# Linear attention in pairs of chunks, and the state space output a half tile later

## What is computed

```python
def gla_chunked(q, k, v, log_a):          # 4 heads, DK 128, DV 256, CHUNK 64
    b = cumsum(log_a) within a chunk
    q_in = qc * exp(b - b_ref);  k_in = kc * exp(b_ref - b)
    o_intra = where(mask, q_in @ k_in.T, 0) @ vc
    q_inter = qc * exp(b);  k_state = kc * exp(b_last - b)
    # over the chunks, one after the other:
    o = q_inter @ state
    state = exp(b_last) * state + k_state.T @ vc
    return o_intra + o
```

## Time and profile before

| | us |
|---|---|
| median of 3 runs (lowest, highest) | 2891.02 (2888.39, 2895.56) |
| the profiled run | 2889.62 |
| its span, first to last instruction | 2887.9 |
| mean granted clock of TensorE | 0.981 |

### The profile page before, as it was taken

One profiled execution on the slowest core, in us unless ns is written; L12 is line 12 of the kernel. 1 busy time (PEld: TensorE's weight loads), 2 busy tenths in 40 slices (PEclk: granted clock), 3 DMA queues, 4 the chain that ended last, 5 costly groups with the idle time before them and its releaser, 6 DMA issues.

```text
span 2887.9 us, 36253 instructions
## 1 busy us (share of the span) xinstructions
PE 2703.7 (94%) x12891; PEld 2135.1 (74%) x12891; DVE 1811.9 (63%) x3282; ACT 953.3 (33%) x1231; POOL 850.7 (29%) x546
## 2 busy tenths in 40 slices
PE   4999899999777999999999999999998999899997
PEld 2455344699656999999999887698666777588875
DVE  5843754899897787878887898530118633360532
ACT  2324232333465223323233222543233233332221
POOL 2100001255201344434444321243112234244442
PEclk8999999999999999999999999999999999899998
DMA  8511334333235899898998897226223532122221
GB/s 333 181 49 61 115 142 142 134 120 121 109 153 210 291 323 314 308 316 309 315 319 303 294 310 260 97 87 122 71 76 121 158 110 87 59 95 95 95 95 59
DMA packets 191363, 502.57 MB, mean 174 GB/s; under 512 B 30800, under 2 KB 79984, under 8 KB 189216
## 3 DMA queue, kind: packets, MB, share of 16 engines
q1 hardware_dynamic: 141680, 317.30, 32.9%
q0 software_dynamic: 49584, 184.04, 18.0%
HBM read 454.42 MB, written 46.86 MB: 174 GB/s over the span
## 4 chain that ended last, share of the span: by engine, by line
PE 63%; issue 17%; DVE 11%; POOL 5%; DMA 1%; DVEq 1%; ACT 1%; POOLq 0%; ACTq 0%
PE psum L1621 18%; PE psum L1608 14%; PE psum L1907 14%; PE psum L541 6%; PE psum L526 6%; POOL l_r L845 4%; DVE arena L1955 2%; DVE arena L1952 2%; DVE look_oh L1952 2%; DVEq L1955 1%; DVE arena L1959 1%; PE psum L1348 1%; PE psum L1914 1%; DVE arena L2298 1%; DVE arena L2299 1%
## 5 line engine op out<-in xcount | busy, mean ns | idle before, releaser
L870 ACT ACTIVATE arena<-psum 128x512 f32<-128x512 f32 (+7 forms) x486 | 327.3, 686 | 1185.4 <-PE psum L1608 386.3
L1952 DVE TENSOR_TENSOR arena<-arena 128x384 f32<-128x384 f32 (+6 forms) x390 | 307.7, 794 | 496.3 <-ACT arena L870 268.8
L845 POOL TENSOR_TENSOR l_r<-arena,l_r 128x1024 fp32r<-128x1024 f32 x144 | 351.6, 2442 | 704.7 <-ACT l_r L485 704.7
L1621 PE MATMUL psum<-e_r,e_r 128*128 128x512 f32 x2304 | 539.0, 390 | 1.8 <-DVE e_r L1952 1.8
L1608 PE MATMUL psum<-e_r,e_r 128*128 128x384 f32 x2048 | 526.2, 337 | 7.9 <-issue 3.5
L1621 PEld LDWEIGHTS psum<-e_r,e_r 128*128 128x128 f32 x2304 | 431.1, 188 | 89.4 <-DVE e_r L1952 2.5
L870 ACT ACTIVATE e_r<-arena 128x1024 fp32r<-128x1024 f32 x256 | 270.3, 1057 | 360.5 <-PE psum L1621 336.1
L1608 PEld LDWEIGHTS psum<-e_r,e_r 128*128 128x128 f32 x2048 | 371.4, 189 | 20.2 <-POOL l_r L817 6.9
L1608 PE MATMUL psum<-e_r,l_r 128*128 128x384 f32 x1024 | 344.4, 336 | 0.0
L829 POOL DMA_INDIRECT arena<-in_up,arena x128 | 163.5, 1277 | 276.3 <-DVE arena L2424 144.6
L829 POOL DMA_INDIRECT arena<-in_down_rows,arena x128 | 164.0, 1281 | 250.8 <-DVE arena L1959 123.6
(11 more groups left out here) (226 smaller groups left out, 3425.4 us busy)
## 6 DMA issues: line engine op xcount, KB each, us to landing
arena<-in_down SPq DMA_DIRECT2D x128, 512.0 KB, 4.3
arena<-in_up SPq DMA_DIRECT2D x128, 512.0 KB, 6.6
arena<-in_w_ada POOLq DMA_DIRECT2D x48, 512.0 KB, 6.7
scratch_gates<-arena SPq DMA_DIRECT2D x12, 2048.0 KB, 6.3
arena<-scratch_gates SPq DMA_DIRECT2D x32, 768.0 KB, 9.5
arena<-in_w_in SPq DMA_DIRECT2D x44, 512.0 KB, 3.3
arena<-in_w_query SPq DMA_DIRECT2D x16, 512.0 KB, 3.3
arena<-in_w_glu SPq DMA_DIRECT2D x16, 512.0 KB, 3.2
```

The lines of the kernel that those rows point to most:

```text
L845: nc.gpsimd.tensor_tensor(rr(lo, 1024, "l"), reg(RING + q % NSLOT * SLOT, 1024), rr(hi, 1024, "l").bitcast(F32), ALU.subtract).then_inc(S[ ...
L870: do(sc.activation(out, in_, f, **kw), sem)
L1621: last = mm(bank(2 * tt_ + hf), rr(w__ + tt_ * P, P), rr(x__ + hf * 512, 512), start=(first and n == 0), stop=(final and n == 2))
L1952: do(v.tensor_tensor(out, a, b, op), sem)
```

## The change

Linear attention takes two chunks of 64 together as one block of 128 (`GDB`, 4 pairs behind the meta tokens). The factors of the reference hold inside a chunk, so a pair's scores are made of three pieces per head: the two diagonal blocks from `QIN` and `KIN`, and the cross block, queries of the second chunk against keys of the first, from `PQ` and `PK`, which carry the factors to and from the chunk's border. Then DVE multiplies the first chunk's keys by the decay of the second, and the second chunk's queries by that of the first (`gla_dec`), so that both serve for the whole pair; the state decays by the product of both (`dec2`). Scores have a step of their own (`gla_scores`), transposes another (`gla_turn`). The output's transposes go to banks 3 and 4. Steps are seven half units apart.

In the state space stretch the output Y, its transposes, the end step and what follows them come one half tile later; on DVE, scan and states come ahead of the ogla tile's product, and the end step behind the states.

```diff
+GDB = [(0, META)] + [(META + 2 * GC * c, 2 * GC) for c in range(T // GC // 2)]
+NGD = len(GDB)
...
-        GLA_A = {3 * c + 1: c for c in range(len(GCH))}
-        GLA_B = {3 * c + 3: c for c in range(len(GCH))}
-        GLA_C = {3 * c + 5: c for c in range(1, len(GCH))}
-        S5_STEP = [{3 * u + n: u for u in range(S5G // GP)} for n in range(8)]
+        GLA_A = {7 * c - 4: c for c in range(1, NGD)}
+        GLA_T = {7 * c - 3 if c else 1: c for c in range(NGD)}
+        GLA_B = {7 * c - 1 if c else 3: c for c in range(NGD)}
+        GLA_C = {7 * c + 1: c for c in range(1, NGD)}
+        S5_STEP = [{3 * u + n: u for u in range(S5G // GP)} for n in (0, 1, 2, 4, 5, 6, 7)]
...
-                    act_(o, bank(5).rearrange("p (m t) -> p m t", m=8)[:, :, 0:L], ACT.Copy, "~o_set")
+                    act_(o, PS[:, 1536:2560].rearrange("p (m t) -> p m t", m=8), ACT.Copy, "~o_set")
...
+            def gla_scores(c):
+
+                t0, L = GDB[c]
+                pe.wait_ge(S["sm"], S.base("sm") + c - 1)
+                for h in range(GLH):
+                    q, k = h * T2 + t0, h * T2 + t0
+                    mm(bank(5)[:, h * P + GC:h * P + L], reg(KIN + k, L), reg(QIN + q + GC, GC), start=True, stop=True)
+                    mm(bank(5)[0:GC, h * P + GC:h * P + L], reg(PK + k, GC), reg(PQ + q + GC, GC), start=True, stop=True)
+                    last = mm(bank(5)[0:GC, h * P:h * P + GC], reg(KIN + k, GC), reg(QIN + q, GC), start=True, stop=True)
+                last.then_inc(S["gla_sc"], 1)
+
+            def gla_turn(c):
+
+                t0, L = GDB[c]
                 if c >= 2:
+                    pe.wait_ge(S["o_set"], S.base("o_set") + c - 1)
+                elif c:
+                    pe.wait_ge(S["vtok"], S.base("vtok") + c)
                 for m in range(8):
                     last = T_(PS[0:L, 1536 + m * P:1536 + (m + 1) * P], reg(PVV + m * T2 + t0, L), P)
+                if c < NGD - 1:
+                    pe.wait_ge(S["ktok"], S.base("ktok") + c)
+                    if c:
+                        pe.wait_ge(S["gla_dec"], S.base("gla_dec") + c)
+                    for h in range(GLH):
+                        last = T_(bank(2)[0:L, h * P:(h + 1) * P], reg(PK + h * T2 + t0, L), P)
                 last.then_inc(S["gla_tr"], 1)
...
-                        mm(o, reg(SM + h * GC, L, L), reg(VTOK + h * DV, DV, L), start=True, stop=False)
+                        mm(o, reg(SM + h * P, P), reg(VTOK + h * DV, DV), start=True, stop=False)
                         last = mm(o, reg(PQ + h * T2 + t0, L), reg(ST + h * DV, DV), start=False, stop=True)
...
-                    last = T_(bank(5)[:, m * GC:m * GC + L], reg(OTOK + m * P, P, L), L)
+                    last = T_(PS[:, 1536 + m * P:1536 + (m + 1) * P], reg(OTOK + m * P, P), P)
...
+            for c, (t0, L) in enumerate(GDB):
                 if c:
                     wait("gla_sc", c)
+                    tt(k1, k1, bc(dec[:, :, 2 * c:2 * c + 1], [P, GLH, GC]), ALU.mult, FREE)
+                    tt(q2, q2, bc(dec[:, :, 2 * c - 1:2 * c], [P, GLH, GC]), ALU.mult, "gla_dec")
...
                 if s % 2 and name == "ogla":
...
-                if s in S5_STEP[1]:
-                    s5_scan(S5_STEP[1][s])
                 if s in S5_STEP[4]:
                     s5_end(S5_STEP[4][s])
-                if s in S5_STEP[2]:
-                    s5_states(S5_STEP[2][s])
```

More of the change, by code:

```diff
@@ L1217, in _ @@
                     c = GLA_B[s]
-                    L = GCH[c][1]
                     wait("x_spilled", 16)
@@ L1772, in gla_a @@
-                if c:
-                    pe.wait_ge(S["sm"], S.base("sm") + c - 1)
-                    if c >= 3:
-                        pe.wait_ge(S["o_set"], S.base("o_set") + c - 2)
-                    for h in range(GLH):
-                        last = mm(bank(5)[0:L, h * GC:h * GC + L], reg(KIN + h * T2 + t0, L), reg(QIN + h * T2 + t0, L),
-                                  start=True, stop=True)
-                    last.then_inc(S["gla_sc"], 1)
+                if c < NGD - 1:
[4 more added lines that the diff above has]
+                        last = T_(bank(2)[0:L, h * P:(h + 1) * P], reg(PK + h * T2 + t0, L), P)
@@ L2546, in _ @@
             tt(K4, K4, E4, ALU.mult, "gq")
-            for c, (t0, L) in enumerate(GCH):
-                wait("gla_tr", c + 1)
-                do(v.tensor_copy(reg(KTOK, 512, L), bank(2)[0:L]), "ktok")
+            dec2 = reg(DEC2, 16).rearrange("p (h c) -> p h c", h=GLH)
+            tt(dec2, dec[:, :, 1:9:2], dec[:, :, 2:9:2], ALU.mult)
+            sm3 = reg(SM, 512).rearrange("p (h q) -> p h q", h=GLH)
+            sc3 = bank(5).rearrange("p (h q) -> p h q", h=GLH)
+            do(v.memset(A[GC:P, SM:SM + 512].rearrange("p (h q) -> p h q", h=GLH)[:, :, 0:GC], 0.0))
+            for c, (t0, L) in enumerate(GDB):
                 if c:
                     wait("gla_sc", c)
-                    tt(reg(SM, 256, L).rearrange("p (h l) -> p h l", h=4),
-                       PS[0:L, 2560:2816].rearrange("p (h l) -> p h l", h=4),
-                       bc(causal[0:L, 0:L].unsqueeze(1), [L, 4, L]), ALU.mult, "sm")
-                if c < len(GCH) - 1:
+                    k1 = reg(PK, 4 * T2).rearrange("p (h t) -> p h t", h=GLH)[:, :, t0:t0 + GC]
+                    q2 = reg(PQ, 4 * T2).rearrange("p (h t) -> p h t", h=GLH)[:, :, t0 + GC:t0 + L]
+                    tt(k1, k1, bc(dec[:, :, 2 * c:2 * c + 1], [P, GLH, GC]), ALU.mult, FREE)
+                    tt(q2, q2, bc(dec[:, :, 2 * c - 1:2 * c], [P, GLH, GC]), ALU.mult, "gla_dec")
+                    if c >= 2:
+                        wait("gla_o", c - 1)
+                    tt(sm3[:, :, GC:L], sc3[:, :, GC:L], bc(causal[:, GC:L].unsqueeze(1), [P, GLH, GC]), ALU.mult, FREE)
+                    tt(sm3[0:GC, :, 0:GC], sc3[0:GC, :, 0:GC], bc(causal[0:GC, 0:GC].unsqueeze(1), [GC, GLH, GC]),
+                       ALU.mult, "sm")
+                if c < NGD - 1:
+                    wait("gla_tr", c + 1)
+                    do(v.tensor_copy(reg(KTOK, 512, L), bank(2)[0:L]), "ktok")
                     wait("gla_st", c + 1)
@@ L2562, in _ @@
                         else:
-                            stt(st, st, dec[:, h, c:c + 1], new, ALU.mult, ALU.add, "st")
-            wait("gla_o", 8)
+                            stt(st, st, dec2[:, h, c - 1:c], new, ALU.mult, ALU.add, "st")
+            wait("gla_o", 4)
             do(v.memset(reg(TT_, 1024), 0.0), "tt_zero")
@@ L2636, in _ @@
                 name, m = half_stage(s)
+                if s in S5_STEP[1]:
+                    s5_scan(S5_STEP[1][s])
+                if s in S5_STEP[2]:
+                    s5_states(S5_STEP[2][s])
                 if s % 2 and name == "ogla":
```

58 lines of the change are left out of this document (27 added, 31 removed).

## The result

The changed kernel takes 2848.93 us (median of 4 runs, 2844.75 to 2850.61), the kernel before, run beside it, 2893.29 (4 runs, 2888.39 to 2895.97): a ratio of 0.9846, 95% interval 0.9828 to 0.9865. It is faster by 44.4 us, or 1.5%. Forecast were 2845 us and a range of 2836 to 2857. The profiled run after took 2850.61 us, with a span of 2848.9.

What follows compares the result with a forecast made beforehand. PE was taken to bound the kernel, busy 94% of the span, with some 19 us of waits in the state space stretch. Terms -34.1 - 9.5 - 1.7 = -45.3 on 2889.6, plus 1.4 for the median, gave 2845 us, range 2836 to 2857.

Steps and rivals of the forecast that it cites:

- PE bounds, linear attention goes only by work: Linear attention stretch, 168.0 us: PE is busy in all of it, so time goes only if PE work goes.
- The term of -34.1: Linear attention: taking chunks in pairs cuts PE work from 75.3 to 41.2 us, bounds -33 to -36.
- a gap behind L1755: Linear attention: no gap from a 128x128 product to 128x64 transposes, read as a sign against a price for width changes.
- Changes of tile width empty the array: Rival, chance 0.08: in the pairs' scores each width change costs 0.15 to 0.17 us, 5 us in all; time 2849.
- The K transposes wait for nothing: Linear attention: K's transposes, now behind two DVE scaling products, cost nothing; up to 3 us if the cover fails.
- The 0.02 for a low clock by that wait: Rival "Slower", chance 0.02: PE falls to the lower clock in linear attention at the new wait before K's transposes.
- The wait passes to S and falls to 8.8: State space stretch: waits for H move from Y to S, most Z2 waits go; 18.3 to 8.8, -9.5 us.
- The wait only moves to S: Rival, chance 0.12, state space stretch: all 18.3 us of waits return, the clock loss too; time 2856.9.
- all waits go: Rival, chance 0.08, state space stretch: the 18.3 us of waits and 5.1 of clock loss vanish; time 2833.5.
- The clock gives 1.7 back: State space stretch: of two clock losses, 1.7 and 3.4 us, the first comes back and the second does not.
- one stretch of low clock, not two: Sign for the new profile, behind the z and r stretch: only one stretch at the lower clock remains.
- The sum: Whole kernel: -34.1 - 9.5 - 1.7 = -45.3 us, giving 2845.

Runs made afterwards that it cites:

- e1: The changed kernel with the state space part taken back, so the attention pairs alone: 2854.94 us, ratio 0.987 to the kernel before.
- e7: The changed kernel with swap product Z1 ahead of output Y in half units that have both: 2844.31 us, ratio 0.984 to the kernel before.
- e5: The changed kernel with a pair's scores grouped by weight width, four 128x128 products first, then eight 128x64: 2845.47 us, ratio 0.9837 to the kernel before.
- e8: The kernel before with output products reordered in pairs of heads, two of 64 rows, then two of 128: 2890.09 us, ratio 0.9991.
- e3: The kernel before with only the later state space steps, old DVE order kept: 2889.16 us, ratio 0.999.
- e4: The kernel before with only the new DVE order, old table of steps kept: 2890.43 us, ratio 0.999.
- e2: The kernel before with the state space part alone (later steps and new DVE order): median 2888.82 us, ratio 0.9986.
- e10: The changed kernel once more, not edited: 2851.22 us in one run.
- e6: The changed kernel with three of norm_o's turns moved on DVE behind the states of the next half tile: 2847.49 us, ratio 0.9844 to the kernel before.
- e9: The changed kernel with scores grouped by weight width and Z1 ahead of Y: median 2842.1 us, ratio 0.982 to the kernel before.

## Why the prediction was right, point by point

*PE bounds, linear attention goes only by work*: right. PE stayed busy in the whole stretch, and the 35.13 us went there; e1 alone has them.

*The term of -34.1*: right in total, within its bounds, by errors that cancelled. The period of a pair, from one group of 12 transposes to the next, is 29.81 us (2036.56 to 2066.37), less seven half units of 2.79: 10.3, where I had 10.9.

| per pair | forecast | measured |
|---|---|---|
| scores | 2.5 | 2.85 |
| 12 transposes, 8 of the output | 1.32, 0.88 | 1.23, 0.79 |
| output products, 16 passes | 3.84 | 3.45 |
| state products | 1.92 | 1.54 (1.73 pass by pass) |
| restarts, the remainder | 0.44 | 0.42 |

The split between passes and changes was wrong. A pass of 256 columns starts 0.216 us behind the one before, with 16, 64 or 128 rows, before and after; I had 0.24 (and 1.84 over 8, my own working, is 0.23). What I had spread over the passes belongs to the changes, 0.14 and not 0.09 each: 16 passes and 8 changes are 3.45 + 1.14 = 4.59, what the earlier trace rows has, and 3.45 is what a pair takes. So of 8 x 4.59 - 4 x 3.45 = 22.9 us some 9 are 64 changes of rows that are gone, and 13.8 the halved number of passes. The state products have no change at their ends any more (0.19 us).

Scores were too cheap: eight changes at 0.14 are 1.1 us, and I put in 0.4 for want of a gap behind L1755. The reading was right, but it was no sign. The 128x64 transposes behind L1755 start 0.23 and 0.11 us apart, as wide ones do; the change stands in the same rows behind them, where the first score starts 0.20 after the last transpose (2035.59) instead of 0.11. The products of Y, with 64 weight columns too, do pay behind a half unit: 0.32 instead of 0.23 (2184.95 after the change). So here transposes with 64 weight columns count as wide, products with 64 do not. At full clock the term is 170.95 to 134.29 us (e7), -36.7, just outside my bounds; one stretch of low clock, 1.7 us, brought it back to -35.1.

*Changes of tile width empty the array* (0.08): its time didn't come, its mechanism did. The eight changes of a pair cost 0.14 us each (e5), 4.5 us over four pairs, where this rival said 0.15 to 0.17 and 5. The output and state products hid that in the total. The Trainium skill (TensorEngine Tiling (Array Packing), Tiling Modes, Key Properties) says that a change of tiling mode drains the engine. The rows agree that there is a price, the same 0.14 for width as for rows (e5, e8). That the array is empty they don't show: by the modelled ends of the profile, the first pass behind a change starts 0.07 us before the last one ahead of it is over (1998.21 against 1998.00 + 0.28).

*The K transposes wait for nothing*: right, no bracket in the timeline. The same for banks 3 and 4 and for r's weights. The 0.02 for a low clock by that wait: there was no wait, but the low clock came in its place at another, behind light products and with PE busy.

*The wait passes to S and falls to 8.8*: right, and nearly number by number: S 1.07, 1.7, 1.0, 3.1, 1.2 forecast, 1.11, 1.64, 1.03, 3.25, 1.01 measured; Z2 0.77 and 0.78. e3 shows the two causes that I named as separate, POOL's subtraction and the end step. "The wait only moves to S" and "all waits go" are both refuted.

*The clock gives 1.7 back*: this step failed. The loss was 4.58 before (5.1 in my working, which took whole stretches and not PE's busy time) and 4.98 after, and "one stretch of low clock, not two" did not come. The argument, a wait of 1.7 being shorter than a harmless one of 1.90, was made from one execution. The loss to be given back was not steady itself: behind the wait at u = 1 the level fell in the kernel before (2.52 us) and e4 (2.49), and not in e1 (2.52) and e8 (2.49). After the change it fell behind the wait of 1.64 or 1.65 in the first profile and e5, and not in e2 and e10; e5 has one more low stretch, behind the wait of 1.11. Of the seven traces of old and new code none has less than one low stretch; and a wait of 3.25 us or more came with one in all seven. The Trainium skill (TensorE: Matmul & The Clock Gate, Part 1: The HAM clock gate) calls the change of clock at a kernel's start run-variable. No run here looks at the start; e10 against the first profile shows the same in the middle of a kernel.

*The sum*: -45.3 forecast, -44.4 by the medians, and -39.0 by the spans (2887.9 to 2848.9), which is -35.13 and -8.48 and the 4.6 us of scatter in code that is the same. That the medians came within 0.9 us of the forecast is luck in part: the attention term gave 1.0 more than forecast and the clock term nothing, within a scatter of several us.

## What to carry to other kernels

On a stream of small products, count the changes of tile shape (rows or weight columns) and price each: here 0.14 us, 3.3 us in all four pairs for grouping the twelve products of a pair by shape. Price the passes and the changes from single starts: a mean over both hides what a change costs. A wait for a chain that runs through another engine moves with the steps; what shortens it is what stands between the links on that engine, and work put off there comes back ahead of the next link (e6). Where the clock takes part, compare stretches as waits, clock loss and rest, and take more than one execution before the clock gets a term. Set total times beside each other at the same mean granted clock: the 29 runs of the kernel before go from 2886.45 to 2888.30 us at 0.983 to 2896.73 to 2899.75 at 0.979.

## What the runs showed of the hardware

- A change between 128x128 and 128x64 weights cost 0.14 us, as did one between 64 and 128 rows (e5, e8): 0.09 at the first pass behind it and 0.05 at the second. From a half unit to float32 transposes with 64 weight columns there was none.
- A float32 pass of 256 columns started 0.216 us behind the one before, with 16, 64 or 128 rows alike (2000.43 and 2013.65 to 2018.61 after the change, 2047.42 before).
- A DVE addition of 128x528 took 0.71 us, and 2.29 to 2.74 when it met POOL's subtraction of 2.4 us (e6, e7).
- The lower clock level came with PE busy throughout and no wait ahead: in the kernel after, e1, e6 and e10 behind the scores of pair 1 and the state products of chunk 0 (1.7 us lost each time). It was absent in e7, with the same code there, and in e5 and e9, with the scores grouped. Whether grouping prevents it can't be told from so few.
- Two kernels had one run of 6450.93 and 8376.75 us among normal ones. Both have a mean granted clock of 1.000 on record; no profile shows what happened in these.
